# The last stage of a hybrid decoder layer: gate product and residual addition on POOL, residual tiles fetched together

## The chip, the cores and the metric

The kernel runs on one core of a Trainium2 chip. The metric is the device time of one execution in microseconds (us); the median of a few executions stands for a kernel. The core's engines have queues of their own: PE (TensorE, matrix products), DVE (VectorE), ACT (ScalarE), POOL (GpSimd) and SP (SyncE). ACT, SP and POOL also issue DMA transfers. Engines wait for each other by semaphores.

## What is computed

One decoder layer for 512 tokens of width 1024. The first half (differential attention beside a Mamba-2 scan) yields `x`. The second half is a mixture of 64 experts. Each token goes through eight of them:

```
h2 = rmsnorm(x, norm2_g) * (1.0 + sc2) + sh2
x  = x + g2 * moe_ffn(h2, ...)          # all float32

moe_ffn: routed = sum over a token's 8 experts of gate[t, e] * (silu(h2 @ w_eg[e]) * (h2 @ w_eu[e])) @ w_ed[e]
         shared = (silu(h2 @ w_sg) * (h2 @ w_su)) @ w_sd
         return routed + shared
```

`g2` is one row of 1024 values, the same for all tokens (the layer's gate). The kernel adds the shared expert, already multiplied by `g2`, to the residual before the experts run, so the last stage has to form `out = x2 + g2 * sum_k w8[t, k] * y[t, k]`, with `x2` the residual that includes the shared expert.

## The kernel before

Up to the last stage the kernel goes through the attention, the scan and the router, then through the 64 experts, one after the other. POOL gathers each expert's tokens by an indirect DMA and scatters the expert's results by another (L589) into the DRAM tensor `y_rows`, eight rows to a token. Nothing of this is touched by the change. The gate is kept in DRAM as `g2_dram` (128 identical rows), the residual as `x2_dram`.

The last stage, functions `fin_pool`, `fin_act` and `fin_vec`, starts when the last scatter has landed (`m_y`). It works on four tiles of 128 tokens, `t` = 0 to 3.

- **ACT** (`fin_act`) issues transfers only. It fetches the gate into `g2f` (L840) while the last expert ends. For each tile it then fetches four pairs of expert rows into `ysum` (L847, 128 x 2048 float32, 1 MB each) and, behind them, the tile's residual into `xfin[:, t]` (L850, 0.5 MB). `ysum` has four buffers, one for each pair, so a pair of tile `t` is fetched when DVE has used the same pair of tile `t - 1`; ACT waits for that on the semaphore `fin_used`. All of ACT's transfers share one DMA queue (q10).
- **DVE** (`fin_vec`) does the arithmetic. For a tile: one `tensor_scalar` (L862) and seven `scalar_tensor_tensor` (L864) for the weighted sum of eight rows in `ofin[:, t % 2]`, then the product with the gate (L869) and the residual addition (L871). Each instruction waits until the one before it has ended. The last one of a tile raises `fin_out`. From tile 2 on the first instruction of a tile waits until the result that was in the same `ofin` buffer has been written out (`out_done0`, `out_done1`).
- **SP** (`sp_moe`, L571) writes `ofin[:, t % 2]` to `out` when `fin_out` says so, and at the end waits for the writes. These transfers are on another DMA queue (q1).
- **POOL** (`fin_pool`) waits for the last scatter and does nothing more.

Two groups of instructions of the scan, far from the last stage, are of use below because they are POOL's only large arithmetic in this kernel: L936 writes `ua` (128 x 1024) as the product of `upper` and a broadcast of `aa`, and L944 multiplies `xs_rows` (128 x 512) in place by a broadcast of `dskip`. DVE's neighbours of them are L1719, L1722 and L1730, all `tensor_tensor` with two operands in SBUF.

Of the kernel before, what the change touches and what calls it, by code (L numbers as in the profile page):

```python
# [24 lines left out]
ALU = mybir.AluOpType  # L25
# [5 lines left out]
NT = T // P  # L31
D = 1024
# [6 lines left out]
TOPK, NG, PG = 8, 8, 8  # L39
# [14 lines left out]
def wait(eng, sem, value):  # L54

    if isinstance(value, int) and value <= 0:
        return
    eng.wait_ge(sem, value)
# [103 lines left out]
def build(nc, x, c, positions, w_ada, b_ada, norm1_g, w_in, q_norm_g, k_norm_g, lambda_qk, subln_g,  # L162
# [23 lines left out]
    x2_dram = dram("x2_dram", (P, NT * D))  # L186
# [141 lines left out]
    xfin = sb("xfin", [P, NT, D])  # L328
    g2f = sb("g2f", [P, D])
    ofin = sb("ofin", [P, 2, D])  # L330

    with ExitStack() as ctx:
        psum = ctx.enter_context(nc.psum_tensor("psum", [P, 8, 512], F32))
        S = {}
# [170 lines left out]
        def hold(eng, sem, value):  # L505

            eng.wait_ge(sem, value).then_inc(S["held"], 1)
# [5 lines left out]
        def extra(eng, e, body):  # L513

            count, n = read_counts(eng, e)
            with eng.If(count > P):
                body(1, n)
            with eng.If(count > 2 * P):
                for j in (2, 3):
                    body(j, n + (j - 1))  # L520
# [54 lines left out]
        def pool_moe(pool, L):  # L575
            pool.wait_ge(S["tok_ready"], 1)
            pool.wait_ge(S["x2_out"], 32)
            pool.wait_ge(S["h2_out"], 16 * NT)
            pool.wait_ge(S["cnt_ready"], 1)

            def gather(e):

                pool.indirect_dma_start(xg[:, e % 3, :], None, h2_rows,  # L583
                                        bass.IndirectOffsetOnAxis(ap=tok_of[:, e * NT:e * NT + 1], axis=0),
                                        bounds_check=T - 1, oob_is_err=False).then_inc(S[f"m_x{e % 3}"], 16)

            def scatter(e):

                pool.indirect_dma_start(y_rows, bass.IndirectOffsetOnAxis(ap=row_of[:, e * NT:e * NT + 1], axis=0),  # L589
                                        yb[:], None, bounds_check=T * TOPK - 1,  # L590
                                        oob_is_err=False).then_inc(S["m_y"], 16)

            def more_rows(e, j, x_):

                nc.gpsimd.tensor_copy(oix[:, 0:1], tok_of[:, bass.ds(e * NT + j, 1)]).then_inc(S["more_idx"], 1)
                hold(pool, S["more_idx"], x_ * 2 + 1)
                pool.indirect_dma_start(xo[:], None, h2_rows, bass.IndirectOffsetOnAxis(ap=oix[:, 0:1], axis=0),
                                        bounds_check=T - 1, oob_is_err=False).then_inc(S["more_x"], 16)

            def more(e):  # L600
                def body(j, x_):
                    o = lambda n: S[f"more_{n}"]
                    more_rows(e, j, x_)
                    nc.gpsimd.tensor_copy(oix[:, 1:2], row_of[:, bass.ds(e * NT + j, 1)]).then_inc(o("idx"), 1)
                    hold(pool, o("idx"), x_ * 2 + 2)
                    hold(pool, o("y"), x_ + 1)
                    pool.indirect_dma_start(y_rows, bass.IndirectOffsetOnAxis(ap=oix[:, 1:2], axis=0), yo[:], None,
                                            bounds_check=T * TOPK - 1, oob_is_err=False).then_inc(o("s"), 16)
                    hold(pool, o("s"), x_ * 16 + 16)
                extra(pool, e, body)  # L610

            for e in range(3):
                gather(e)
            for e in range(NE + 1):
                if e + 3 < NE:
                    pool.wait_ge(S["xt_ps"], e + 1)
                    gather(e + 3)
                if e:
                    pool.wait_ge(S["y_ev"], e)
                    scatter(e - 1)  # L620
                if e < NE:
                    more(e)
            fin_pool(pool)

        GU = (2, 3, 7)

# [79 lines left out]
        def act_moe(a, A, L):  # L706
# [26 lines left out]
            def it(e, par, turn):  # L733
# [23 lines left out]
                if whole:  # L757
# [10 lines left out]
                    extra(a, e, body)  # L768
            iterations(it, a, NE + 1)
            fin_act(a)  # L770

        def vec_moe(v, L):
# [30 lines left out]
            def it(e, par, turn):  # L803
# [15 lines left out]
                if whole:  # L819
# [8 lines left out]
                    extra(v, e, body)  # L828
            iterations(it, v, NE + 1)
            fin_vec(v)  # L830


        def fin_pool(pool):

            pool.wait_ge(S["m_y"], 16 * NE)

        def fin_act(a):

            a.wait_ge(S["dn_ps"], NE)
            a.dma_start(g2f[:], g2_dram).then_inc(S["fin_x"], 16)  # L840
            a.wait_ge(S["m_y"], 16 * NE)
            ys = y_rows.rearrange("(t p k) d -> t p k d", p=P, k=TOPK)
            for t in range(NT):
                for pair in range(TOPK // 2):

                    wait(a, S["fin_used"], (t - 1) * (TOPK + 1) + 2 * pair + 2)
                    a.dma_start(ysum[:, pair], ys[t, :, 2 * pair:2 * pair + 2, :]).then_inc(S[f"fin_y{pair}"], 16)  # L847

                wait(a, S["fin_used"], t * (TOPK + 1))
                a.dma_start(xfin[:, t, :], x2_dram[:, t * D:(t + 1) * D]).then_inc(S["fin_x"], 16)  # L850

        def fin_vec(v):

            V = nc.vector
            for t in range(NT):
                o_ = ofin[:, t % 2, :]
                if t >= 2:
                    v.wait_ge(S[f"out_done{t % 2}"], 16 * (t // 2))
                for k in range(TOPK):
                    v.wait_ge(S[f"fin_y{k // 2}"], 16 * (t + 1))  # L860
                    if k == 0:
                        ins = V.tensor_scalar(o_, ysum[:, k // 2, k % 2, :], w8[:, t, k:k + 1], None, ALU.mult)  # L862
                    else:
                        ins = V.scalar_tensor_tensor(out=o_, in0=ysum[:, k // 2, k % 2, :], scalar=w8[:, t, k:k + 1], in1=o_,  # L864
                                                     op0=ALU.mult, op1=ALU.add)
                    ins.then_inc(S["fin_used"], 1)
                    v.wait_ge(S["fin_used"], t * (TOPK + 1) + k + 1)
                v.wait_ge(S["fin_x"], 16 * (t + 2))
                V.tensor_tensor(o_, o_, g2f[:], ALU.mult).then_inc(S["fin_used"], 1)  # L869
                v.wait_ge(S["fin_used"], (t + 1) * (TOPK + 1))  # L870
                V.tensor_tensor(o_, o_, xfin[:, t, :], ALU.add).then_inc(S["fin_out"], 1)  # L871


        @blk.sync
# [17 lines left out]
        def _(pool):  # L892
# [32 lines left out]
            for s in steps:  # L925
# [49 lines left out]
                if kind_ == "h2":  # L975
                    pool.wait_ge(S["m_lo"], KD)
                    pool.dma_start(wr[:], w_router[0].rearrange("(p k) n -> p k n", p=P)).then_inc(S["wr_in"], 16)
                    pool_route(pool, L)
            pool_moe(pool, L)


# [848 lines left out]
```

## Time and profile before

| | us |
|---|---|
| median of 3 runs | 2066.68 |
| lowest, highest | 2063.21, 2070.07 |
| the profiled execution, device time | 2074.8 |
| its span, first to last instruction | 2072.8 |
| last stage in it: from the issue of the first `ysum` transfer to the end of the span | 2014.53 to 2072.8 |
| granted TensorE clock, mean | 0.89 |

All times in views are counted from the start of the span. The device time of the profiled execution lies 2.0 us over its span. A row of a timeline is: start, duration, engine, line, operation, output and inputs, count if several were merged (the duration then reaches from the first to the end of the last), and in brackets how long the engine had been idle before and what ended this. A transfer's row shows its issue by ACTq or SPq; when it landed stands in the rows on transfers.

### The profile page before, as it was taken

The numbers are of one execution on the slowest core, as the hardware profiler recorded it, in microseconds if no ns is written. First come the engines' busy times: TensorE is split into PE (matmuls) and PEld (weight loads), VectorE is DVE, ScalarE is ACT, GpSimd is POOL, SyncE is SP. The second block draws the span as 40 slices with busy tenths as digits, with TensorE's granted clock in tenths as the row PEclk, the third lists the DMA queues.
The fourth block names the chain that finished last, engine by engine and source line by source line (L and its number), as shares of the span: only waits on it lengthen the run. The fifth ranks groups of instructions, "written<-read, shape, count | busy, mean of one in ns | idle before, by whom it ended". The sixth has DMA issues, their size and how long they took to land.

```text
span 2072.8 us, 23077 instructions
## 1 busy us (share of the span) xinstructions
PE 1651.7 (80%) x7242; PEld 1276.1 (62%) x7243; DVE 1330.2 (64%) x1717; ACT 926.2 (45%) x1132; POOL 314.2 (15%) x282
## 2 busy tenths in 40 slices
PE   6697797799698798796975737899999669999860
PEld 1484685687476485584764625777777557777750
DVE  2486476546637657666446556788888337887859
ACT  2226425423233232322332225677777347777740
POOL 1000000000200202002100071123233122223210
PEclk9698998899699798897898867999999789999985
DMA  8110220244033050240520138899999449999948
GB/s 267 67 62 21 69 74 21 102 134 151 0 122 101 21 179 24 61 163 0 189 73 20 41 115 293 296 349 342 345 352 372 159 183 330 334 335 335 326 180 365
DMA packets 126064, 361.42 MB, mean 174 GB/s; under 512 B 21164, under 2 KB 31600, under 8 KB 115344
## 3 DMA queue, kind: packets, MB, share of 16 engines
q1 hardware_dynamic: 98352, 295.20, 41.0%
q0 software_dynamic: 22688, 45.29, 5.9%
q10 hardware_dynamic: 4928, 19.78, 2.4%
q8 instruction: 44, 0.72, 0.1%
q14 instruction: 52, 0.43, 0.1%
HBM read 352.18 MB, written 43.66 MB: 191 GB/s over the span
## 4 chain that ended last, share of the span: by engine, by line
PE 51%; DMA 24%; DVE 11%; ACT 6%; issue 5%; POOL 2%; POOLq 1%; ACTq 0%; SPq 0%; DVEq 0%
DMA y_rows<-yb,row_of 21%; PE psum L1188 13%; PE psum L1189 13%; PE psum L1190 13%; ACT yb L756 3%; PE psum L1388 2%; POOL slot_table L493 2%; PE psum L1210 1%; DVE ofin L864 1%; PE psum L1368 1%; PE psum L1342 1%; PE psum L1314 1%; DMA ysum<-y_rows 1%; PE psum L1399 1%; DMA rawm<-in_w_exp_down 1%
## 5 line engine op out<-in xcount | busy, mean ns | idle before, releaser
L784 DVE TENSOR_TENSOR ring<-rawm,ring 128x2048 fp32r<-128x2048 f32 x192 | 433.8, 2287 | 85.9 <-ACT ring L715 85.9
L715 ACT ACTIVATE ring<-rawm 128x2048 fp32r<-128x2048 f32 x192 | 355.4, 1908 | 31.1 <-DMA g_dram<-g2b 15.9
L1188 PE MATMUL psum<-ring,xT 128*128 128x512 f32 x528 | 219.5, 416 | 49.6 <-DVE xT L792 49.1
L1485 DVE TENSOR_TENSOR hl<-raw,hl 128x2048 fp32r<-128x2048 f32 x59 | 134.4, 2291 | 143.8 <-ACT hl L996 143.3
L1189 PE MATMUL psum<-ring,xT 128*128 128x512 f32 x528 | 211.9, 401 | 0.0
L1190 PE MATMUL psum<-ring,xT 128*128 128x512 f32 x528 | 211.5, 401 | 0.3 <-issue 0.3
L1188 PE MATMUL psum<-hl,hT 128*128 128x512 f32 x416 | 165.1, 397 | 11.2 <-DVE hT L1762 11.2
L996 ACT ACTIVATE hl<-raw 128x2048 fp32r<-128x2048 f32 x59 | 112.0, 1910 | 129.0 <-PE psum L1190 93.6
L1189 PE MATMUL psum<-hl,hT 128*128 128x512 f32 x416 | 162.9, 392 | 0.0
L1190 PE MATMUL psum<-hl,hT 128*128 128x512 f32 x416 | 162.8, 391 | 0.0
L1188 PEld LDWEIGHTS psum<-ring,xT 128*128 128x128 f32 x528 | 102.9, 195 | 84.3 <-DVE xT L792 41.1
L589 POOL DMA_INDIRECT y_rows<-yb,row_of x64 | 78.3, 1224 | 447.6 <-ACT yb L756 432.6
L583 POOL DMA_INDIRECT xg<-h_rows,tok_of x64 | 114.6, 1790 | 79.0 <-issue 63.8
L1188 PE MATMUL psum<-hT,hl 128*128 128x512 f32 x320 | 126.1, 394 | 0.0
L1190 PE MATMUL psum<-hT,hl 128*128 128x512 f32 x320 | 124.6, 389 | 0.0
L1189 PE MATMUL psum<-hT,hl 128*128 128x512 f32 x320 | 124.6, 389 | 0.0
L1190 PEld LDWEIGHTS psum<-ring,xT 128*128 128x128 f32 x528 | 102.6, 194 | 23.0
L1189 PEld LDWEIGHTS psum<-ring,xT 128*128 128x128 f32 x528 | 103.1, 195 | 19.9
L1188 PE MATMUL psum<-ring,aT 128*128 128x512 f32 x264 | 109.9, 416 | 4.1 <-DVE aT L796 4.1
L756 ACT ACTIVATE yb<-psum 128x1024 f32<-128x1024 f32 x64 | 65.8, 1028 | 104.9 <-DMA y_rows<-yb,row_of 88.1
L792 DVE TENSOR_TENSOR xT<-psum,xT 128x1024 fp32r<-128x1024 f32 x66 | 80.8, 1225 | 40.2 <-ACT xT L718 40.1
L1190 PE MATMUL psum<-ring,aT 128*128 128x512 f32 x264 | 105.0, 398 | 0.0
(370 smaller groups left out, 3092.0 us busy)
## 6 DMA issues: line engine op xcount, KB each, us to landing
rawm<-in_w_exp_gate SPq DMA_DIRECT2D x128, 512.0 KB, 7.9
rawm<-in_w_exp_up SPq DMA_DIRECT2D x128, 512.0 KB, 10.7
rawm<-in_w_exp_down SPq DMA_DIRECT2D x64, 1024.0 KB, 6.8
raw<-in_w_in SPq DMA_DIRECT2D x36, 1024.0 KB, 5.2
raw<-in_w_ada SPq DMA_DIRECT2D x24, 1024.0 KB, 5.2
ysum<-y_rows ACTq DMA_DIRECT2D x16, 1024.0 KB, 9.0
raw<-in_w_branch_b SPq DMA_DIRECT2D x8, 1024.0 KB, 5.3
raw<-in_w_branch_a SPq DMA_DIRECT2D x4, 1024.0 KB, 5.1
```

The lines of the kernel that those rows point to most:

```text
L493: pool.indirect_dma_start(slot_table, bass.IndirectOffsetOnAxis(ap=addr8i[:, t, k:k + 1], axis=0), tokid[:, t, k:k + 1], None).then_inc(S[ ...
L583: pool.indirect_dma_start(xg[:, e % 3, :], None, h2_rows, bass.IndirectOffsetOnAxis(ap=tok_of[:, e * NT:e * NT + 1], axis=0), bounds_check ...
L589: pool.indirect_dma_start(y_rows, bass.IndirectOffsetOnAxis(ap=row_of[:, e * NT:e * NT + 1], axis=0), yb[:], None, bounds_check=T * TOPK - ...
L715: A(ring[:, slot, 1, :], rawm[slot][:], ACT.Copy).then_inc(S["m_hi2"], 1)
L756: A(yb[:], psum[:, 5:7].rearrange("p b n -> p (b n)"), ACT.Copy).then_inc(S["y_ev"], 1)
L784: TT(ring[:, slot, 0, :], rawm[slot][:], ring[:, slot, 1, :].bitcast(F32), ALU.subtract).then_inc(S["m_lo2"], 1)
L792: return TT(xT[:, par, :, 1, :], psum[:, 0:2].rearrange("p b (k t) -> p (b k) t", t=P), xT[:, par, :, 0, :].bitcast(F32), ALU.subtract)
L996: A(hl[:, u["m"] % HL, 0, :], raw[:, u["n"] % RAW], ACT.Copy).then_inc(S["hi_done"], 1)
L1188: M(dst, lhs(0), rhs(0), start=first, stop=False)
L1189: M(dst, lhs(0), rhs(1), start=False, stop=False)
L1190: return M(dst, lhs(1), rhs(0), start=False, stop=last)
L1485: TT(h_[:, 1, :], r, h_[:, 0, :].bitcast(F32), ALU.subtract).then_inc(S["lo_done"], 1)
```

## The change

Three things are changed, all in the last stage:

- POOL gets the gate product and the residual addition of each tile. It waits until `g2f` and all four residual tiles have landed (`fin_x` at 80) and DVE has done the tile's eight instructions, does the two operations in place on `ofin[:, t % 2]`, the second behind the first by its own semaphore (`L`), and raises `fin_out`.
- ACT issues the four residual transfers one after the other directly behind the first tile's four pairs, with no wait. They were issued one behind each tile's pairs, and the later three waited for DVE.
- DVE keeps the eight weighted-sum instructions. `fin_used` counts 8 a tile instead of 9.

```
+        def fin_pool(pool, L):
             pool.wait_ge(S["m_y"], 16 * NE)
+            for t in range(NT):
+                o_ = ofin[:, t % 2, :]
+                pool.wait_ge(S["fin_x"], 16 * (NT + 1))
+                pool.wait_ge(S["fin_used"], (t + 1) * TOPK)
+                L(nc.gpsimd.tensor_tensor(o_, o_, g2f[:], ALU.mult))
+                nc.gpsimd.tensor_tensor(o_, o_, xfin[:, t, :], ALU.add).then_inc(S["fin_out"], 1)
...
         def fin_act(a):
...
-                    wait(a, S["fin_used"], (t - 1) * (TOPK + 1) + 2 * pair + 2)
+                    wait(a, S["fin_used"], (t - 1) * TOPK + 2 * pair + 2)
                     a.dma_start(ysum[:, pair], ys[t, :, 2 * pair:2 * pair + 2, :]).then_inc(S[f"fin_y{pair}"], 16)
-                wait(a, S["fin_used"], t * (TOPK + 1))
-                a.dma_start(xfin[:, t, :], x2_dram[:, t * D:(t + 1) * D]).then_inc(S["fin_x"], 16)
+                if t == 0:
+                    for j in range(NT):
+                        a.dma_start(xfin[:, j, :], x2_dram[:, j * D:(j + 1) * D]).then_inc(S["fin_x"], 16)
...
         def fin_vec(v):
...
-                    v.wait_ge(S["fin_used"], t * (TOPK + 1) + k + 1)
-                v.wait_ge(S["fin_x"], 16 * (t + 2))
-                V.tensor_tensor(o_, o_, g2f[:], ALU.mult).then_inc(S["fin_used"], 1)
-                v.wait_ge(S["fin_used"], (t + 1) * (TOPK + 1))
-                V.tensor_tensor(o_, o_, xfin[:, t, :], ALU.add).then_inc(S["fin_out"], 1)
+                    v.wait_ge(S["fin_used"], t * TOPK + k + 1)
```

On ACT's queue, at its end: `ysum` and `xfin` are the destinations in SBUF. Before:

```order
L840 DMA g2f<-g_dram 128x1024 [waits dn_ps]
L847 DMA ysum<-y_rows 128x2048 [waits m_y]
L847 DMA ysum<-y_rows 128x2048 x3
L850 DMA xfin<-x_dram 128x1024
L847 DMA ysum<-y_rows 128x2048 [waits fin_used] x4
L850 DMA xfin<-x_dram 128x1024 [waits fin_used]
```

After:

```order
L846 DMA g2f<-g_dram 128x1024 [waits dn_ps]
L853 DMA ysum<-y_rows 128x2048 [waits m_y]
L853 DMA ysum<-y_rows 128x2048 x3
L857 DMA xfin<-x_dram 128x1024 x4
L853 DMA ysum<-y_rows 128x2048 [waits fin_used] x12
```

The three later residual transfers moved ahead of all the pairs of tiles 1 to 3.

On POOL's queue, at its end, behind the last expert's scatter. Before:

```order
L589 DMA y_rows<-yb,row_of 4096x1024 [waits y_ev]
L332 UNCONDITIONAL_BRANCH [waits m_y]
```

After:

```order
L589 DMA y_rows<-yb,row_of 4096x1024 [waits y_ev]
L840 TENSOR_TENSOR ofin<-ofin,g2f 128x1024 [waits fin_used,fin_x,m_y]
L841 TENSOR_TENSOR ofin<-ofin,xfin 128x1024 [waits pool_line]
L840 TENSOR_TENSOR ofin<-ofin,g2f 128x1024 [waits fin_used,fin_x]
L841 TENSOR_TENSOR ofin<-ofin,xfin 128x1024 [waits pool_line]
```

Eight operations of 128 x 1024 moved from DVE to here, two for each tile (the first two tiles are shown).

## Rows read from the trace of the kernel before

**Rows 1.** Timeline of the last stage, ACT's, SP's and DVE's rows.

```profile
2014.53 2.01 ACTq L847 DMA_DIRECT2D ysum<-y_rows  x4
...
2019.37 0.75 DVE L862 TENSOR_SCALAR ofin<-ysum,w 128x1024 f32<-128x1024 f32 x1 [14.09 <-DMA ysum<-y_rows]
...
2029.85 1.23 DVE L869 TENSOR_TENSOR ofin<-ofin,g2f 128x1024 f32<-128x1024 f32 x1
...
2032.25 0.75 DVE L862 TENSOR_SCALAR ofin<-ysum,w 128x1024 f32<-128x1024 f32 x1
2032.36 37.75 SPq L571 DMA_DIRECT2D out<-ofin  x4
2033.03 9.32 DVE L864 SCALAR_TENSOR_TENSOR ofin<-ysum,w,ofin 128x1024 f32<-128x1024 f32 x7
...
2044.79 0.74 DVE L862 TENSOR_SCALAR ofin<-ysum,w 128x1024 f32<-128x1024 f32 x1
...
2054.84 1.23 DVE L869 TENSOR_TENSOR ofin<-ofin,g2f 128x1024 f32<-128x1024 f32 x1
...
2057.24 0.75 DVE L862 TENSOR_SCALAR ofin<-ysum,w 128x1024 f32<-128x1024 f32 x1
2058.02 9.21 DVE L864 SCALAR_TENSOR_TENSOR ofin<-ysum,w,ofin 128x1024 f32<-128x1024 f32 x7
2067.26 1.22 DVE L869 TENSOR_TENSOR ofin<-ofin,g2f 128x1024 f32<-128x1024 f32 x1
2068.52 1.22 DVE L871 TENSOR_TENSOR ofin<-ofin,xfin 128x1024 f32<-128x1024 f32 x1
```

**Rows 2.** Stretches: length, busy of PE, PEld, DVE, ACT, POOL; PEclk, DMA share, GB/s.

```profile
2016.20:2065.20 49.00, 0.00 (x0) 0.00 (x0) 44.07 (x37) 0.00 (x0) 0.00 (x0) 0.50 1.00 414
2026.90:2028.60 1.70, 0.00 (x0) 0.00 (x0) 1.63 (x3) 0.00 (x0) 0.00 (x0) 0.50 1.00 340
```

**Rows 3.** Transfers from 1995 us on: count, KB each, median us from issue to landing.

```profile
ysum<-y_rows ACTq DMA_DIRECT2D x16, 1024.0 KB, 9.0
xfin<-x_dram ACTq DMA_DIRECT2D x4, 512.0 KB, 9.9
out<-ofin SPq DMA_DIRECT2D x4, 512.0 KB, 7.5
```

**Rows 4.** Issue and landing of the first `xfin` (2016.5 to 2017 us).

```profile
L850 ACTq DMA_DIRECT2D xfin<-x_dram x1: 462/462/462, 2016.6 to 2016.6; - x1
...
DMA to landing us min/median/max: 11.9/11.9/11.9
```

**Rows 5.** Issue and landing of the last `ysum` pair (2054 to 2058 us).

```profile
L847 ACTq DMA_DIRECT2D ysum<-y_rows x1: 326/326/326, 2054.8 to 2054.8; - x1
...
DMA to landing us min/median/max: 9.7/9.7/9.7
```

**Rows 6.** POOL's two arithmetic lines: ns min/median/max, first and last start, shapes.

```profile
L936 POOL TENSOR_TENSOR ua<-upper,aa x16: 1891/1895/1917, 458.7 to 961.4; 128x1024 f32<-128x1024 f32 x16
L944 POOL TENSOR_TENSOR xs_rows<-xs_rows,dskip x16: 1041/1955/2024, 526.8 to 971.3; 128x512 f32<-128x512 f32 x16
```

**Rows 7.** Timeline in the scan, 664 to 670 us: POOL beside DVE.

```profile
664.72 1.90 POOL L936 TENSOR_TENSOR ua<-upper,aa 128x1024 f32<-128x1024 f32 x1 [110.31 <-PE psum L1368]
664.89 2.28 DVE L1719 TENSOR_TENSOR cv<-xs_rows,dtdec 128x512 f32<-128x512 f32 x1
667.09 1.21 DVE L1722 TENSOR_TENSOR lm<-lm,cbm 128x1024 f32<-128x1024 f32 x1
...
667.25 1.95 POOL L944 TENSOR_TENSOR xs_rows<-xs_rows,dskip 128x512 f32<-128x512 f32 x1 [0.63 <-DVE cv L1719]
668.23 1.52 DVE L1730 TENSOR_TENSOR cv<-cv,expo 128x512 f32<-128x512 f32 x1
```

**Rows 8.** The same lines where the other engine is idle, 688 to 693 us.

```profile
689.09 0.68 DVE L1730 TENSOR_TENSOR cv<-cv,expo 128x512 f32<-128x512 f32 x1
...
691.25 0.69 DVE L1719 TENSOR_TENSOR cv<-xs_rows,dtdec 128x512 f32<-128x512 f32 x1
692.02 1.04 POOL L944 TENSOR_TENSOR xs_rows<-xs_rows,dskip 128x512 f32<-128x512 f32 x1 [4.73 <-DVE cv L1719]
```

More of the change, by code:

```diff
@@ L622, in pool_moe @@
                     more(e)
-            fin_pool(pool)
+            fin_pool(pool, L)
         GU = (2, 3, 7)
@@ L830, in vec_moe @@
             fin_vec(v)
-        def fin_pool(pool):
+        def fin_pool(pool, L):
             pool.wait_ge(S["m_y"], 16 * NE)
+            for t in range(NT):
[4 more added lines that the diff above has]
+                nc.gpsimd.tensor_tensor(o_, o_, xfin[:, t, :], ALU.add).then_inc(S["fin_out"], 1)
         def fin_act(a):
```

## The prediction

> **What bounds the kernel now.** The change touches only what follows the last scatter, so I read the timeline of that stretch first [rows 1]. DVE starts at 2019.37 and ends at 2068.52 + 1.22 = 2069.74, and the timeline shows it busy nearly throughout: tile 1 starts at 2032.25, tile 2 at 2044.79, tile 3 at 2057.24, 12.5 us each. From the first instruction of a tile to the end of the eighth are 2054.84 - 2044.79 = 10.05 us; the gate product and the residual addition take the other 2.5. Read alone, this says that DVE is the bound and that 2.5 us a tile are to be had.
>
> The stretches say something else [rows 2]: from 2016.2 to 2065.2 the DMA engines are busy with a share of 1.00 at 414 GB/s. What goes through in these 49 us is 16 pairs of 1.05 MB, four residual tiles and three results of 0.52 MB, 20.4 MB in all, and 20.4 / 0.414 = 49.4 us. So both are full. The transfers show how narrow it is [rows 3, 5]: the last pair is issued at 2054.8 and lands 9.7 us later, at 2064.5. DVE's seventh instruction of tile 3 needs it; it starts five steps of 1.32 us behind 2058.02, at 2064.6. The DMA queue is 0.1 us ahead of DVE. Taking work off DVE can't bring the last pair sooner.
>
> **Part 1: the residual tiles first.** The first residual lands 11.9 us after 2016.6, at 2028.5 [rows 4]. Now three more follow it ahead of tile 1's first pair, in the same queue. While the first one was moved the rate was 340 GB/s [rows 2]: 0.52 / 0.34 = 1.54 us each; at 414 it would be 1.27. So the fourth lands at 2032.3 to 2033.1; I take 2032.8. Tile 1's first pair is behind it, 1.05 / 0.414 = 2.5 us: 2035.3. DVE is through with tile 0 at 2029.85 and idles until then. Before, it started tile 1 at 2032.25. The bytes are the same in all, so the transfers that this delays are made up by the residuals that no longer come later.
>
> **Part 2: what an operation costs on POOL.** The trace has no POOL product of 128 x 1024 with two full operands. The nearest rows [rows 6]: L936, 128 x 1024 with a broadcast operand, 1.90 us; L944, 128 x 512 in place like the new ones, 1.04 us at its shortest, twice which is 2.08. I take 2.08, the in-place form, and 1.90 as the other end. Two of them with a gap of 0.1 us are 4.3 us; DVE did them in 2.5. The GPSIMD Engine Reference of the Trainium skill (3.1, side-by-side cycle accounting) gives 4497 ns for a two-operand product of 2048 float32, so by estimate 2.25 us for 1024; no row here has that form, and by it the sum below would be about 2.5 us longer.
>
> **Part 3: POOL and DVE beside each other.** This carries the forecast. In the scan [rows 7], L1719 on DVE starts 0.17 us behind a POOL product and takes 2.28 us, where it takes 0.69 with POOL idle [rows 8]: it ends at 667.17, 0.56 us after POOL's end at 664.72 + 1.90 = 666.62. DVE stood still for POOL's whole operation. The other way round, L944 is issued at 667.25 while L1722 runs until 668.30, and ends at 669.20: 0.90 us after it, where it takes 1.04 alone. L1730, which DVE wants to start at 668.23, then takes 1.52 us instead of 0.68 [rows 8]. So the two don't run side by side when both read two operands from SBUF; who waits gets its turn at the other's next end. The seven `scalar_tensor_tensor` of a tile have two SBUF operands, as the POOL operations have. A POOL operation that waits its turn costs DVE its duration less 0.2 us (1.52 - 0.68 = 0.84 for one of 1.04). Two of 2.08 cost 2 x 1.88 = 3.8 us a tile. DVE is freed of 2.5 us and loses 3.8.
>
> **The sum**, against the profiled execution:
> - Tile 0: POOL starts when the fourth residual has landed, 2032.8 + 0.1, and ends two operations later at 2037.2. DVE's first instruction of tile 1 could start at 2035.3, in the middle of POOL's second operation, and waits: the tile counts from about 2037.1 (before: 2032.25, so +4.8).
> - Tile 1: 10.05 us, undisturbed: ends at 2047.1. Its last pair is due by the queue at 2035.3 + 3 x 2.5 = 2042.8 and perhaps 1 us for the first result, so it doesn't hold DVE up.
> - Tile 2: 10.05 + 3.8, since POOL's work on tile 1 falls into it: 2061.0. Tile 3: the same, 2074.8.
> - Then POOL's two operations for tile 3, with nothing beside them: 0.1 + 4.3, 2079.1. The write is issued and lands as before.
>
> 2079.1 against 2069.74 is +9.4 us; with operations of 1.90 us it is 4.8 - 0.4, 13.45 a tile and 4.0 at the end: 2077.7, +8.0. Nothing ahead of 2016 changes. On the median that is 2066.68 + 9.3 = **2076.0 us** (with one decimal less than the terms have), 0.45% more. Tiles 2 and 3 now need 13.8 us each for some 4.7 MB, which take 11.4 by the DMA: the queue, full before, is no longer the bound.
>
> **Waits that are added.** SP's writes wait for POOL; only they are behind that wait. The result of tile 1 is issued when POOL has gone through two turns: 0.75 for DVE's first instruction, 2.08, 1.3 for the next, 2.08, about 6.2 us after 2047.1, at 2053.3; with 7.5 us to land [rows 3] it is out at 2060.8. DVE's first instruction of tile 3 waits for just that and is due at 2061.0. It is a near thing, and costs nothing by the sum.
>
> **Rivals.**
> - *POOL and DVE run side by side.* Then the DMA queue is the bound, as before: the last pair lands at 2064.5, two instructions of 1.3 end at 2067.2 as in the trace, and 4.4 us of POOL follow instead of 2.5: +1.9, 2068.6 us, not slower by what can be measured. For it: the sum of the bytes is exact. Against it: rows 7. It decides if `scalar_tensor_tensor` does not keep POOL out as `tensor_tensor` does; the trace shows no such pair.
> - *DVE is the only bound, and the queue catches up.* If the queue had slack that the early issues hide, and the residuals delay nothing: 2029.85 + 3 x 10.05 + 4.4 = 2064.4, -5.3 us, 2061.3. Against it: DMA share 1.00 and both findings above. This is the most the change could bring.
> - *POOL doesn't get its turn between DVE's instructions.* Then tile 1's two operations run only when DVE has finished tile 2 (2047.1 + 10.05, 2057.2), the result is out 4.4 + 2.6 to 7.5 us later, and DVE's tile 3 starts at 2064 to 2069 instead of 2061; it ends at 2074 to 2079, POOL then still has tile 2's and tile 3's work, 8.6: +13 to +18. For it: DVE's instructions follow each other within 0.03 us. Against it: L944 took its turn in just such a gap at 668.3.
>
> **How the numbers follow.** Turns taken between POOL and DVE: 0.67, itself +7 to +12.5 (operations of 1.90 to 2.25 us, and 1.5 us of scatter between medians). Side by side: 0.14. POOL kept out: 0.09. DVE alone: 0.05. Something else, half of it on each side: 0.05. The range from 2068 to 2081 takes in the first but for its upper edge, the second, and the low end of the third. About 0.3%, 6.2 us, is what a measurement of this kernel can tell from no change. Slower by more: 0.67 x 0.88 + 0.09 + 0.02 = 0.70. Within: 0.67 x 0.12 + 0.14 + 0.03 and half of the fourth, 0.27. Faster: 0.03.
>
> **What the profile after would show.** Right: in tiles 2 and 3 two of DVE's eight instructions take about 3.1 us instead of 1.29, each ending 1.1 us or so after a POOL operation; DVE idle from 2029.9 to about 2037, DMA share below 1 from 2048 on; POOL operations of 1.9 to 2.1 us when alone (tile 3) and up to 3.3 when they wait; POOL's end 9 us later than DVE's end before. Wrong: all DVE instructions at 1.29 and DVE idle for `ysum` (side by side); POOL operations of ten us (kept out); operations of tile 3 at 2.3 us or more (only the size is off); the fourth residual far from 2032.8 (part 1).

## The result and the profile after

| | median, us | lowest, highest | ratio, 95% interval |
|---|---|---|---|
| before, beside the first measurement | 2067.6 | 2063.21, 2070.5 | |
| after, first measurement (6 runs) | 2083.94 | 2082.21, 2087.82 | 1.0081 [1.0066, 1.0096] |
| before, beside the second measurement | 2072.28 | 2066.8, 2079.27 | |
| after, second measurement (12 runs) | 2084.91 | 2071.59, 2091.79 | 1.0053 [1.0037, 1.0070] |

The change makes the kernel slower, by 0.8% in the first measurement and 0.5% in the second. The forecast was 2076.0 us, 0.45% slower, with 2081 as the upper end: the direction held, the measured time lies 7.9 us above the forecast and 2.9 us above the range.

The last stage can be read more finely in a trace than in medians. I call its length the time from the issue of the first `ysum` transfer to the end of the span: 58.3 us before (2014.53 to 2072.8), 70.4 us after (2010.63 to 2081.0), 12.1 more. First the timeline of it in the kernel after (columns as in [rows 1], with which it is to be compared; L869 and L871 are DVE's weighted sum, L840 and L841 POOL's product and addition):

```profile
2010.63 1.97 ACTq L853 DMA_DIRECT2D ysum<-y_rows  x4
2012.63 2.04 ACTq L857 DMA_DIRECT2D xfin<-x_dram  x4
...
2018.05 7.89 DVE L871 SCALAR_TENSOR_TENSOR ofin<-ysum,w,ofin 128x1024 f32<-128x1024 f32 x6 [0.47 <-DMA ysum<-y_rows]
2028.60 2.34 POOL L840 TENSOR_TENSOR ofin<-ofin,g2f 128x1024 f32<-128x1024 f32 x1 [20.15 <-DMA xfin<-x_dram]
2031.01 2.34 POOL L841 TENSOR_TENSOR ofin<-ofin,xfin 128x1024 f32<-128x1024 f32 x1
2031.06 2.85 DVE L869 TENSOR_SCALAR ofin<-ysum,w 128x1024 f32<-128x1024 f32 x1 [5.12 <-DMA ysum<-y_rows]
2033.38 43.21 SPq L571 DMA_DIRECT2D out<-ofin  x4
2033.93 9.21 DVE L871 SCALAR_TENSOR_TENSOR ofin<-ysum,w,ofin 128x1024 f32<-128x1024 f32 x7
2043.18 0.75 DVE L869 TENSOR_SCALAR ofin<-ysum,w 128x1024 f32<-128x1024 f32 x1
2043.29 2.84 POOL L840 TENSOR_TENSOR ofin<-ofin,g2f 128x1024 f32<-128x1024 f32 x1 [9.94 <-DVE ofin L871]
2043.97 13.12 DVE L871 SCALAR_TENSOR_TENSOR ofin<-ysum,w,ofin 128x1024 f32<-128x1024 f32 x7
2046.21 3.20 POOL L841 TENSOR_TENSOR ofin<-ofin,xfin 128x1024 f32<-128x1024 f32 x1
2057.24 2.34 POOL L840 TENSOR_TENSOR ofin<-ofin,g2f 128x1024 f32<-128x1024 f32 x1 [7.83 <-DVE ofin L871]
2058.78 1.34 DVE L869 TENSOR_SCALAR ofin<-ysum,w 128x1024 f32<-128x1024 f32 x1 [1.69 <-DMA out<-ofin]
...
2060.16 11.17 DVE L871 SCALAR_TENSOR_TENSOR ofin<-ysum,w,ofin 128x1024 f32<-128x1024 f32 x7
2071.47 2.34 POOL L840 TENSOR_TENSOR ofin<-ofin,g2f 128x1024 f32<-128x1024 f32 x1 [9.15 <-DVE ofin L871]
2073.89 2.34 POOL L841 TENSOR_TENSOR ofin<-ofin,xfin 128x1024 f32<-128x1024 f32 x1
```

In order: DVE has nothing to do from 2025.9 to 2031.06, because tile 1's first pair is behind four residual tiles. Its first instruction of tile 1 then takes 2.85 us instead of 0.75, since POOL is in its second operation. Tile 1 runs undisturbed (seven instructions in 9.21 us, as in [rows 1]). In tile 2 the same seven take 13.12 us. One of them alone, from the timeline of DVE in a narrower stretch:

```profile
2043.97 3.24 DVE L871 SCALAR_TENSOR_TENSOR ofin<-ysum,w,ofin 128x1024 f32<-128x1024 f32 x1
```

It starts at 2043.97, while POOL's product has the turn until 2046.13, and ends 1.1 us behind that. It takes 3.24 us for 1.285 undisturbed, so the turn costs DVE 1.96 us.

Beside the kernel before, the 12.1 us are made up of this: DVE's sum of tile 1 ends 4.7 us later (32.5 us from the start of the stage, 27.8 before), from there to the end of the sum of tile 2 it takes 1.5 us more and to that of tile 3 1.8 more, product and addition of tile 3 take 2.4 more, and what follows them 1.7 more.

The DMA engines, full from end to end before [rows 2], are no longer so (columns as there; the last but one is the DMA share):

```profile
2050.00:2055.00 5.00, 0.00 (x0) 0.00 (x0) 4.86 (x5) 0.00 (x0) 0.00 (x0) 0.50 0.94 324
2055.00:2060.00 5.00, 0.00 (x0) 0.00 (x0) 3.27 (x3) 0.00 (x0) 2.68 (x2) 0.50 1.00 382
2060.00:2065.00 5.00, 0.00 (x0) 0.00 (x0) 4.89 (x4) 0.00 (x0) 2.32 (x1) 0.50 0.62 257
```

There is room in the first and the third stretch, not in the second. The last pair of `ysum` is issued at 2057.1 and lands 7.3 us later, at 2064.4; the instruction that needs it starts at 2068.7. So it is there 4.3 us ahead of its use, where it was 0.1 us ahead before.

The end of the span holds something that I had no term for. POOL's last operation ends at 2076.23 and the last result has landed by 2078.9, but the span ends at 2081.0. Among the rows of the program's last line, where the engines end and meet, are POOL's and SP's DRAIN (a sequencer instruction; ns min/median/max, then the start). After:

```profile
L332 POOLq DRAIN  x1: 6967/6967/6967, 2073.9 to 2073.9; - x1
...
L332 SPq DRAIN  x1: 7/7/7, 2079.1 to 2079.1; - x1
```

Before:

```profile
L332 POOLq DRAIN  x1: 4568/4568/4568, 2014.7 to 2014.7; - x1
```

Behind POOL's last work the DRAIN takes 4.6 us: to 2080.8 after (it is issued beside the last operation), long before the end in the kernel before.

### The profile page after: what moved, and what is told of

Its sections match the earlier page's. It is cut to its first block, busy times and chain, and to the rows that moved or that the text cites. A ratio compares the mean times of both kernels' runs of the same rounds, so it can differ in the third digit from the quotient of the medians.

```text
span 2081.0 us, 23078 instructions
## 1 busy us (share of the span) xinstructions
PE 1646.0 (79%) x7242; PEld 1274.5 (61%) x7243; DVE 1329.9 (64%) x1709; ACT 926.5 (45%) x1132; POOL 339.2 (16%) x290
## 4 chain that ended last, share of the span: by engine, by line
PE 51%; DMA 24%; DVE 10%; ACT 6%; issue 5%; POOL 2%; POOLq 1%; ACTq 0%; SPq 0%; DVEq 0%
DMA y_rows<-yb,row_of 20%; PE psum L1191 13%; PE psum L1193 13%; PE psum L1192 13%; ACT yb L756 2%; PE psum L1391 2%; POOL slot_table L493 2%; PE psum L1213 1%; PE psum L1371 1%; PE psum L1345 1%; DVE ofin L871 1%; DMA rawm<-in_w_exp_down 1%; PE psum L1317 1%; DMA ysum<-y_rows 1%; PE psum L1402 1%
## 5 line engine op out<-in xcount | busy, mean ns | idle before, releaser
L1191 PE MATMUL psum<-ring,xT 128*128 128x512 f32 x528 | 221.8, 420 | 48.2 <-DVE xT L792 47.3
L1193 PE MATMUL psum<-ring,xT 128*128 128x512 f32 x528 | 214.5, 406 | 0.2 <-issue 0.2
L1192 PE MATMUL psum<-ring,xT 128*128 128x512 f32 x528 | 214.3, 406 | 0.0
L1191 PEld LDWEIGHTS psum<-ring,xT 128*128 128x128 f32 x528 | 104.7, 198 | 82.2 <-DVE xT L792 38.3
L1193 PEld LDWEIGHTS psum<-ring,xT 128*128 128x128 f32 x528 | 104.0, 197 | 23.5
L1192 PEld LDWEIGHTS psum<-ring,xT 128*128 128x128 f32 x528 | 104.5, 198 | 20.7
```

The lines of the kernel that those rows point to most:

```text
L1191: M(dst, lhs(0), rhs(0), start=first, stop=False)
L1192: M(dst, lhs(0), rhs(1), start=False, stop=False)
L1193: return M(dst, lhs(1), rhs(0), start=False, stop=last)
```

## Experiments

All ratios are to the kernel before on the same chip, from 12 runs of the variant (6 for e2 and e6) and 29 of the kernel before; a stage's length is read from one trace. e3, e5, e9 and e11 leave out or alter a part of the result. "Stage" gives the issue of the first `ysum` transfer, the end of the span, and the difference.

| run | stage, us | more than 58.4 | ratio, 95% interval | median less median of before, us |
|---|---|---|---|---|
| e0 before again | 2011.61 to 2070.0, 58.4 | 0 | 1.0002 [0.9986, 1.0018] | -1.1 |
| e1 residuals first | 2016.71 to 2079.0, 62.3 | +3.9 | 1.0036 [1.0022, 1.0051] | +5.2 |
| e2 POOL alone | 2013.90 to 2081.1, 67.2 | +8.8 | 1.0058 [1.0035, 1.0081] | +10.1 |
| e3 sums only | 2010.69 to 2066.8, 56.1 | -2.3 | 0.9985 [0.9970, 0.9999] | -2.9 |
| e4 after again | 2019.68 to 2090.0, 70.3 | +11.9 | 1.0053 [1.0037, 1.0070] | +12.6 |
| e5 POOL writes only | 2015.96 to 2082.5, 66.5 | +8.1 | 1.0037 [1.0022, 1.0052] | +7.9 |
| e6 four results | 2013.14 to 2083.2, 70.1 | +11.7 | 1.0061 [1.0043, 1.0080] | +12.3 |
| e7 last tile on DVE | 2010.64 to 2076.6, 66.0 | +7.6 | 1.0028 [1.0012, 1.0044] | +6.2 |
| e8 early fetch | 2012.33 to 2070.7, 58.4 | 0 | 1.0013 [1.0001, 1.0025] | +1.3 |
| e9 early fetch, sums only | 2013.19 to 2065.1, 51.9 | -6.5 | 0.9971 [0.9954, 0.9988] | -6.3 |
| e10 first product on ACT | 2013.93 to 2069.9, 56.0 | -2.4 | 0.9991 [0.9977, 1.0005] | -2.1 |

### Nothing changed (e0), the change again (e4)

> The kernel before, unchanged, for a second trace of it and a ratio with nothing in it. In the two traces at hand the last stage (first ysum issue to the end of the span) is 58.3 us before (2014.53 to 2072.8) and 70.4 us after (2010.63 to 2081.0), 12.1 more, while the medians differ by 16.3. Theory 1: all of the difference is in the last stage and the rest is scatter of what lies ahead of it, which is the same program; then this run has a ratio within 0.9985 to 1.0015, a last stage of 58.3 plus or minus 0.5, and a first ysum issue that differs from 2014.5 by several us. Theory 2: something ahead of the last stage became slower too; then the first ysum issue of this run lies near or under 2010, earlier than in the trace after, relative to its own time.

> The changed kernel once more, for a second trace and a second ratio beside the other variants. The stage from the first ysum issue to the end of the span was 70.4 us in its trace, against 58.3 and 58.4 in two traces before: +12.1. Theory 1 (all of it is in the last stage): ratio 1.0058, the first ratio of 1.0081 was partly scatter. Theory 2 (3 to 5 us more are lost ahead of the stage in the timed runs): ratio 1.008 again. In both the stage is 70.4 in the trace.

The stage repeats to 0.1 us in both kernels, 58.3 and 58.4, 70.4 and 70.3. What lies ahead of it does not: the same program reached it at 2010.63 in one execution and at 2019.68 in another. The 14 traces of this document reach it at 2010.7 to 2016.7 (the kernel before and those built on it) and at 2010.6 to 2019.7 (the changed kernel and those built on it), so one kind has no visible lead. The 29 runs of the kernel before beside e0 alone spread from 2066.3 to 2079.8 us, the 12 of e4 from 2071.6 to 2091.8. The second ratio of the change, 1.0053, is what 12 us of stage give (1.0058); the first, 1.0081, is 16 us. Over the variants the third column and the last differ by 1.4 us at most. So the stage accounts for the change. The 4 us by which the first measurement goes beyond it are most simply scatter, but their cause stays open: what lay ahead of the stage in those six runs can't be shown, as only one has a trace.

### The two parts apart (e1, e2)

The edit of e1, on the kernel before:

```
-                wait(a, S["fin_used"], t * (TOPK + 1))
-                a.dma_start(xfin[:, t, :], ...)
+                if t == 0:
+                    for j in range(NT):
+                        a.dma_start(xfin[:, j, :], ...)
...
-                v.wait_ge(S["fin_x"], 16 * (t + 2))
+                v.wait_ge(S["fin_x"], 16 * (NT + 1))
```

> The order of the transfers alone: all four residual tiles behind tile 0's pairs, DVE does all the arithmetic as before. Theory A (both DVE and the queue are full, so a late start is not made up): DVE starts tile 1 about 20.6 us after the first ysum issue instead of 17.7, and goes on at 12.5 us a tile; last stage 58.3 + 2.7 to 3.1 = 61.2 us, ratio 1.0014. Theory B (slack in DVE's tiles takes it up): last stage 58.3, ratio 1.000. Theory C (the first tile hides it): DVE starts tile 1 as before.

It came out by theory A, and 1 us longer than it said. Who waited for whom in that trace (total, times, longest):

```profile
DVE ofin L870 <- DMA xfin<-x_dram: 2.5, 1, 2.5
...
DVE ofin L865 <- DMA ysum<-y_rows: 2.0, 4, 0.6
```

DVE's product of tile 0 waits 2.5 us for all four residuals (tile 1 starts 20.4 us into the stage instead of 17.7), and then three pairs of tile 1, delayed, come one by one just behind DVE, which costs up to 0.6 us each and 1.5 in all (the fourth wait of the second row is in tile 0, as before the change). Neither is made up later.

e2 is the changed kernel with the order of transfers of before:

```
-                if t == 0:
-                    for j in range(NT):
-                        a.dma_start(xfin[:, j, :], ...).then_inc(S["fin_x"], 16)
+                wait(a, S["fin_used"], t * TOPK)
+                a.dma_start(xfin[:, t, :], ...).then_inc(S[RES[t][0]], 16)      # a semaphore for each tile
```

> The move to POOL alone: the residual tiles are fetched one behind each tile's pairs as before, POOL waits for each one by itself. From the trace after: an undisturbed tile on DVE takes 10.05 us, one with both POOL operations in it 14.0. Theory A (POOL and DVE take turns): DVE's tile 0 ends 15.3 us after the first ysum issue, tiles 1, 2 and 3 take 14 each: 57.4; POOL's two operations 4.8: 62.2; then POOL's DRAIN at the end of the program, 4.6 as after its last operation in the trace after: last stage 66.8 us, 8.5 more than before, ratio 1.004. Theory B (the lengthening in the trace after came from the order of the transfers): last stage about 60, ratio 1.001.

It came out by theory A: 67.2 us against 66.8. The move to POOL alone is 8.8 of the 12 us, though it takes 2.5 us of work off DVE in every tile. The parts are 3.9 + 8.8 = 12.7 against 11.9 together. One difference between the traces fits this: in the full change much of tile 0's POOL work falls into DVE's idle time and costs DVE 2.1 us (2.85 for 0.75), while in e2 it costs 3.1 (1.86 for 0.75, and 11.17 for 9.21).

### What POOL's operation does to DVE (e5, e11)

```
-                L(nc.gpsimd.tensor_tensor(o_, o_, g2f[:], ALU.mult))
-                nc.gpsimd.tensor_tensor(o_, o_, xfin[:, t, :], ALU.add).then_inc(S["fin_out"], 1)
+                flat_x = xfin[:].rearrange("p t d -> p (t d)")
+                wait(pool, S["fin_out"], t)
+                L(nc.gpsimd.memset(flat_x[:, 0:2688], 0.0))
+                nc.gpsimd.memset(flat_x[:, 0:2688], 0.0).then_inc(S["fin_out"], 1)
```

> POOL's two operations of a tile are replaced by two memsets of 128 x 2688, chosen to take about the same 2.34 us but reading nothing (gate product and residual addition are left out). Everything else is as in the changed kernel. Theory A (POOL keeps DVE out only while POOL reads SBUF): DVE's instructions all take 1.29, DVE's tile is 10.05 us, tiles 2 and 3 are held to about 11.2 by the queue or by the output wait; stage 70.4 less 2 x 3 = 64 us. Theory B (any POOL operation on SBUF keeps DVE out): 70.4 us, with DVE instructions of 3.2 us as in the changed kernel. Theory C (the lengthening of DVE's instructions is not from POOL): 70.4 too, with long instructions away from the memsets.

The groups of instructions in that stage (count, busy, mean ns, idle before):

```profile
L873 DVE SCALAR_TENSOR_TENSOR ofin<-ysum,w,ofin 128x1024 f32<-128x1024 f32 x28 | 36.0, 1285 | 1.4 <-DMA ysum<-y_rows 0.5
L843 POOL MEMSET xfin<- 128x2688 f32 x4 | 10.2, 2550 | 0.2
L871 DVE TENSOR_SCALAR ofin<-ysum,w 128x1024 f32<-128x1024 f32 x4 | 9.5, 2366 | 18.0 <-DMA ysum<-y_rows 18.0
```

The same in the changed kernel:

```profile
L871 DVE SCALAR_TENSOR_TENSOR ofin<-ysum,w,ofin 128x1024 f32<-128x1024 f32 x28 | 41.9, 1495 | 1.4 <-DMA ysum<-y_rows 0.5
```

The 28 two-operand instructions take 1285 ns on average, as undisturbed ones do, and this takes in those of tiles 2 and 3 that run beside the second memset, a POOL operation of the same length that only writes. So it is POOL's reading that kept them out: that part of theory A holds, and B and C fall. (The memset also writes another buffer than `ofin`; but in [rows 7] L936 holds up L1719, and the two share no buffer.) But the stage is 66.5, not 64. The missing part is the first instruction of a tile, `tensor_scalar` with one operand, 2.4 us on average over the four tiles where it takes 0.75, with 2.8 to 2.96 in tiles 1 to 3: it is kept out by the memset too. The timeline at tile 2 of that run shows both kinds, the first beside the first memset, the second beside the second:

```profile
2048.37 2.96 DVE L871 TENSOR_SCALAR ofin<-ysum,w 128x1024 f32<-128x1024 f32 x1
2048.45 2.34 POOL L842 MEMSET xfin<- 128x2688 f32 x1 [9.90 <-DVE ofin L873]
2050.84 2.76 POOL L843 MEMSET xfin<- 128x2688 f32 x1
2051.37 1.28 DVE L873 SCALAR_TENSOR_TENSOR ofin<-ysum,w,ofin 128x1024 f32<-128x1024 f32 x1
```

The Trainium skill (SBUF — State Buffer, "SBUF: two separate sides") states this split: the pair of ports shared by VectorE and GpSimd is an exclusive lock, taken on VectorE's side by operations in a 2-port mode, or by those with two SBUF inputs, the latter only against a GpSimd operation that reads SBUF. By that rule both of POOL's real operations keep out the `scalar_tensor_tensor`, and the memset doesn't; the traces agree, with 3.24 us for 1.285 beside the first and 1.28 beside the second. The `tensor_scalar` has one SBUF input, so by that rule it is kept out only in a 2-port mode. No row shows the mode; what the traces show is 2.85 us for 0.75 beside POOL's addition and 2.96 beside the memset.

e11 changed the form of POOL's product (one run, with its trace):

```
-                L(nc.gpsimd.tensor_tensor(o_, o_, g2f[:], ALU.mult))
+                by_h = o_.rearrange("p (h d) -> p h d", d=HP)
+                L(nc.gpsimd.tensor_tensor(by_h, by_h, g2f[:, 0:16].unsqueeze(2).to_broadcast([P, 16, HP]), ALU.mult))
```

> The changed kernel, but POOL's first operation of a tile multiplies by 16 values of the gate, each broadcast over 64 columns (so the product is not the layer's; the form is that of the scan's in-place product, 128 x 512, 1.04 us). Its second operation is unchanged, with two full operands. In the trace after both forms with full operands take 2.34 us alone. Theory A (a broadcast operand makes a POOL product cheaper; this is why the two rows of the scan, 1.90 and 2 x 1.04, were too low for the last stage): the first operation takes 1.9 to 2.1 us in tile 3, the second 2.34. Theory B (the operand's form doesn't matter; the last stage's operations are slower for another reason, such as their place in memory or transfers running beside them): both 2.34.

Its rows for tile 3, POOL alone:

```profile
2077.05 1.90 POOL L841 TENSOR_TENSOR ofin<-ofin,g2f 128x1024 f32<-128x1024 f32 x1 [7.83 <-DVE ofin L872]
2079.03 2.34 POOL L842 TENSOR_TENSOR ofin<-ofin,xfin 128x1024 f32<-128x1024 f32 x1
```

It came out by theory A: a broadcast operand makes the product 0.44 us cheaper. That is why both rows that I could price from [rows 6], each with a broadcast, were too low. The same trace gives a second price of a turn: DVE's seven instructions of tile 2 take 12.68 us, against 13.12 with the longer product and 9.21 undisturbed. Both prices fit one rule, the duration of POOL's operation less 0.38 us: 1.96 + 1.52 = 3.48 for the measured 3.47, and 2 x 1.96 = 3.92 for 3.91.

The estimate of 2.25 us, worked out from the GPSIMD Engine Reference of the Trainium skill (3.1, for an addition of 2048 float32), was nearer to the measured 2.34, which product and addition both take.

### Waits and the end of the program (e6, e7)

e6 gives each tile an `ofin` buffer of its own and drops the waits on `out_done`:

```
-    ofin = sb("ofin", [P, 2, D])
+    ofin = sb("ofin", [P, NT, D])
...
-                if t >= 2:
-                    v.wait_ge(S[f"out_done{t % 2}"], 16 * (t // 2))
```

> The changed kernel with four ofin buffers instead of two, so that no tile waits for an earlier result to be written out. In the trace after, DVE waited 1.7 us for that ahead of tile 3. Theory A (the wait was its own cost): 1.7 us less, stage 68.7. Theory B (turns: in the wait POOL did its first operation for tile 2 undisturbed, and without the wait DVE pays for it in tile 3 instead, 14.0 us against 12.5): DVE ends at most 0.3 us earlier, stage 70.1 to 70.4.

It came out by theory B: 70.1 us. The wait of 1.7 us in the first trace (the result of tile 1 took 9.3 us to land there) was no cost of its own, as POOL did its product for tile 2 in it. In e4, with two buffers, the result landed in 5.3 us, DVE didn't wait at all, and the stage was as long.

e7 leaves tile 3's product and addition on DVE:

```
-            for t in range(NT):
+            for t in range(NT - 1):                 # POOL
...
+            v.wait_ge(S["fin_out"], NT - 1)         # DVE, behind tile 3's sum
+            V.tensor_tensor(o_, o_, g2f[:], ALU.mult).then_inc(S["fin_used"], 1)
+            v.wait_ge(S["fin_used"], NT * TOPK + 1)
+            V.tensor_tensor(o_, o_, xfin[:, NT - 1, :], ALU.add).then_inc(S["fin_out"], 1)
```

> POOL does tiles 0 to 2 as in the changed kernel, DVE does the gate product and the addition of tile 3 itself. In the trace after POOL's last operation ended at 2076.2, the last result had landed at 2078.9, and POOL's DRAIN at the program's end went on to 2080.9, 4.6 us after its last operation; in both traces before, this DRAIN takes 4.57 us long before the end. Theory A (that DRAIN is a fixed tail behind POOL's last work): DVE's tile ends at 60.7 + 2.5 = 63.2 us after the first ysum issue, 3.0 for the write as before, stage 66.2 us; POOL's DRAIN is over at 57 and costs nothing. 4.2 less than after: 2.3 by faster operations, 1.9 by the hidden DRAIN. Theory B (no such tail): 68.1.

It came out by theory A: 66.0 us against 66.2. Two rows of its end:

```profile
2072.30 1.22 DVE L879 TENSOR_TENSOR ofin<-ofin,xfin 128x1024 f32<-128x1024 f32 x1
```

```profile
L332 POOLq DRAIN  x1: 7830/7830/7830, 2060.1 to 2060.1; - x1
```

POOL's DRAIN is over at 2067.9, DVE's work at 2073.5, and the span ends 3.1 us after DVE, as before the change. In the five other traces in which POOL works last (e2, e4, e5, e6 and e11) its DRAIN takes 6.95 to 6.97 us from beside the last operation, as in the first trace after.

### Is there anything to gain by relieving DVE? (e3, e8, e9, e10)

e3 is the kernel before without product and addition (its eight instructions, and all transfers, stay). e8 is the kernel before with the residual and the gate fetched earlier, by SP, into buffers of the expert ring that are no longer used:

```
+            sp.wait_ge(S["dn_ps"], NE - 2)
+            sp.dma_start(g2f[:], g2_dram).then_inc(S["fin_x"], 16)
+            sp.dma_start(flat(xfin[:]), x2_dram).then_inc(S["fin_x"], 16)
```

e9 is both at once.

> The kernel before without the gate product and the residual addition (they are left out, so the result is the weighted sum alone); a one-column memset takes the place of one count. All transfers as before. Theory A (the queue is full): the last pair still lands about 50 us after the first ysum issue, two instructions of 1.3 follow; last stage 58.3 - 2.5 = 55.8 us, ratio 0.9988, and DVE idles for ysum by some 7 us. Theory B (DVE alone was the bound): 4 x 2.5 less, 48.3 us, ratio 0.995.

> The kernel before with gate and residual fetched by SP during the last two experts, into buffers that the experts have left, so that the 2.1 MB of residual are off the queue in the last stage; DVE does all the arithmetic. Theory A (two limits of equal size: queue and DVE): relieving the queue alone brings nothing, stage 58.3 plus or minus 0.4, ratio 1.000, and the last pair lands 4 us ahead of its use instead of 0.1. Theory B (the queue alone was the bound): 5 us less, 53.3.

> Early fetch as in e8 and DVE without gate product and residual addition (left out, as in e3). e3 alone gave 2.2 us, e8 should give nothing. Theory A (both limits moved together): the queue moves 16.8 + 1.6 MB at 0.414 MB a us, 44.4 us, from 1.7 us on: the last pair lands at 46.1, two instructions of 1.3 and 3.0 for the write: stage 51.7 us, 6.6 less than before, ratio 0.9968. Theory B (gains add up): 56.1.

All three came out by theory A, within 0.3 us: 56.1, 58.4 and 51.9. Waits of DVE in e3:

```profile
DVE ofin L863 <- DMA ysum<-y_rows: 16.3, 4, 13.0
DVE ofin L865 <- DMA ysum<-y_rows: 4.7, 7, 1.1
```

(13.0 us of the first row are the wait ahead of the first tile, which every kernel has.) Ten us of work taken off DVE (four times 2.5) shorten the stage by 2.3; the rest comes back as waits for `ysum`. Five us taken off the queue shorten it by nothing. Together they give 6.5, not the sum. The kernel before stands on two limits of the same height, and even a perfect move of the product and the addition would have brought at most 2.3 us, 0.1%. e8's ratio, 1.0013 [1.0001, 1.0025], lies just above 1 with an unchanged stage. If that is more than scatter, it is lost ahead of the stage, where e8 fetches earlier; no run shows it.

e10 is a complete kernel that takes off both: early fetch, and the first product of each tile on ACT, which idles in this stage:

```
+                nc.scalar.activation(ofin[:, t % 2, :], ysum[:, 0, 0, :], ACT.Copy, scale=w8[:, t, 0:1]).then_inc(...)
...
-                for k in range(TOPK):                # DVE
+                for k in range(1, TOPK):
```

> A complete kernel. Gate and residual fetched early as in e8; the first row of tile 0 by a transfer of its own; and each tile's first product (w8 times row 0) on ACT instead of DVE, written to ofin while DVE ends the tile before. Theory A (ACT's product does not keep DVE out, as POOL's did): DVE's tile is 7 x 1.32 + 2.5 = 11.7 us, the queue's 11.3; DVE starts at about 5.3, waits 0.8 for the second pair: 5.3 + 0.8 + 4 x 11.7 + 3.0 = 55.9 us, 2.4 less than before, ratio 0.9988. Theory B (ACT's operation delays DVE as POOL's did): DVE's instructions beside it take up to 1 us longer, stage 58 to 60.

It came out by theory A, 56.0 us against 55.9. ACT's operation and DVE's beside it:

```profile
2052.71 1.23 DVE L877 TENSOR_TENSOR ofin<-ofin,g2f 128x1024 f32<-128x1024 f32 x1
2053.14 1.15 ACT L861 ACTIVATE ofin<-ysum,w 128x1024 f32<-128x1024 f32 x1 [10.49 <-DVE ofin L874]
2053.97 1.23 DVE L879 TENSOR_TENSOR ofin<-ofin,xfin 128x1024 f32<-128x1024 f32 x1
```

DVE's instruction takes the same 1.23 us with ACT beside it. The stage is 2.4 us shorter than before; the ratio, 0.9991 [0.9977, 1.0005], can't tell that from nothing.

## Where the prediction was right, and why it was wrong

All times here are counted from the first `ysum` issue (forecast: less 2014.53; measured: the first trace after, less 2010.63).

| step of the sum | forecast | measured |
|---|---|---|
| the fourth residual is there, POOL starts | 18.4 | 18.0 |
| end of DVE's tile 1 | 32.6 | 32.5 |
| tile 2, with POOL's two turns | 13.8 | 13.95 |
| tile 3, the same | 13.8 | 14.2 (13.95 in e4) |
| POOL's two operations for tile 3, with gaps | 4.4 | 4.9 |
| from there to the end of the span | 3.1 | 4.8 |
| stage | 67.6 | 70.4 |

The mechanism was right: the residuals delay tile 1, the engines take turns, and the stage is longer for it. The size was not, for two reasons. Of the 7.9 us between 2076.0 and the measured 2083.94, 2.8 are in the stage, and the last item of the sum has 1.7 of them. The other 5.1 lie between medians, in a term of 1.5.

- **The step that failed** is the last item of the sum, "the write is issued and lands as before". The write did (2.6 us from issue to landing in both traces); the program's end no longer followed from it. Where the forecast has 3.1 us from POOL's end to the end of the span, the trace has 4.8: POOL's DRAIN, 4.6 us after its last operation, now ends last, 1.7 us later than the write would have let it. The prediction had no term for it. With tile 3 left on DVE the 3.1 us are back (e7).
- **The scatter** between medians was put at 1.5 us. The stage was 2.8 us longer than summed, which by itself gives 2078.8 us, inside the range; the first measurement lies 5.1 us higher. Of these, 0.9 are the median of the kernel before, which moved from 2066.68 (3 runs) to 2067.6 (6 runs). The cause of the other 4.2 stays open. The second measurement's ratio, 1.0053, would have put the time at 2077.6 us, inside the range: which side of 2081 a measurement falls on is a matter of luck with a scatter of this size. The two ratios of this same change differ by 0.0028, nearly 6 us.
- **Part 1** (order of the transfers) held for where tile 1 starts (forecast 20.8 us into the stage, measured 20.4). That the delayed transfers "are made up" did not hold by itself: in e1 the pairs of tile 1 cost 1.5 us of waits, and the order alone costs 3.9 us.
- **Part 2** (what an operation costs on POOL) was mis-sized: 2.08 us, measured 2.34 (e11 shows why). In the tiles it hardly shows, because a turn costs DVE the operation's duration less 0.38 us, not less 0.2: 1.96 against 1.88. At the end it shows in full, 0.5 us. The prediction's remark that operations of 2.25 us would make the sum 2.5 us longer doesn't follow from its own terms: eight operations count, 0.17 us more each, which is 1.4 us.
- **Part 3** (turns between POOL and DVE) held: in tile 2 DVE loses 3.9 us for the 2.5 that it is freed of. e2 shows it without the new order of transfers, and e5 that for the two-operand instructions it goes with POOL's reading. That the one-operand `tensor_scalar` of tile 1 waits as well was put into the sum with no row behind it; it came out (2.85 us for 0.75), but by luck.
- **The added wait** on the result of tile 1 was called near and free. It did come up, 1.7 us in one trace and none in the other, and was free (e6).
- **The rivals.** Side by side fell by every trace; POOL kept out fell as well, each of its operations waited for one DVE instruction at most; that DVE was the only bound fell by e3.

## What to carry to other kernels

Before moving two-operand work from DVE to POOL, look at what DVE does at the same time: if that reads two operands from SBUF too, the two engines take turns, and an operation that costs DVE 1.23 us costs it 1.96 us when POOL does it (in this kernel, which also has a one-operand `tensor_scalar` held up in the same way). ACT took an operation off DVE with no such price. When a trace shows both an engine and the DMA queue full, price the relief of each alone before counting on it; here the first gave 2.3 of 10 us and the second nothing. And count what an engine does at the end of the program behind its last work, if it did its last work early before.

## What the runs showed of the hardware beyond what was expected

- POOL's DRAIN at the end of the program lasts 4.6 us beyond its last work: after an addition (2076.23 to 2080.8), and 4.57 us when it had only waited for a scatter.
- A broadcast operand makes a POOL product of 128 x 1024 float32 take 1.90 us instead of 2.34.
- A POOL memset of 128 x 2688 (2.34 us) leaves DVE's `scalar_tensor_tensor` at 1.285 us and holds up its `tensor_scalar` (up to 2.96 us for 0.75).
- A turn costs DVE's `scalar_tensor_tensor` the duration of POOL's operation less 0.38 us, for operations of 2.34 us (1.96) and of 1.90 us (1.51 in e11).
- The last stage repeats to 0.1 us, while the start of it in the same program was 9 us apart in two executions.
